# Masked columns left out of the power products of a chunked RWKV-7 inverse

## The chip, the cores and the metric

The kernel runs on one core of a Trainium2 chip. The metric is the device time of one launch in microseconds, as the median of the runs. Three runs of the kernel before took 1457.06 to 1458.89 us, with a median of 1458.34 us.

## The reference, cut to what matters

The reference is a chain of transformer layers over 256 tokens with 1024 features. The part that is changed is the RWKV-7 time mix of the first layer: 16 heads of 64 features, each with a state that is updated token by token.

```python
def step(state, inp):
    r_t, w_t, k_t, v_t, a_t, b_t = inp
    sa = jnp.einsum('bhvk,bhk->bhv', state, a_t)
    state = (state * w_t[:, :, None, :] + sa[..., None] * b_t[:, :, None, :]
             + v_t[..., None] * k_t[:, :, None, :])
    return state, jnp.einsum('bhvk,bhk->bhv', state, r_t)
```

The kernel does it in 4 chunks of 64 tokens. Within a chunk, what the tokens add to one another through `sa` is a triangular system I - A, where A is 64x64 and strictly triangular. A to the power 64 is zero, so the inverse is the product of (I + A)(I + A^2)(I + A^4) up to (I + A^32).

## The kernel before, in words

The 16 heads are worked off as 8 pairs. Of a pair, one head has partitions 0 to 63 ("upper") and the other has partitions 64 to 127 ("lower"). A tile of a pair holds 4 chunks of 64 columns, so it is 128x256.

The inverse has six levels (`power_level`, from L841). `P` is the matrix and `Q` its transpose. P is strictly upper triangular and Q strictly lower triangular.

- Level 0 squares P and Q (P = Q'P and Q = P'Q, in banks ps4 and ps5).
- Levels 1 to 3 square both again, and also multiply the running sum Z by the power (`times_z`, bank ps6). VectorE adds the product to Z (`add_z`, L2016 to L2027). ScalarE copies the new powers out of PSUM (`take_powers`, L1465 to L1473).
- Level 4 squares only Q, and multiplies Z.
- Level 5 only multiplies Z, for the upper head into bank 6 and for the lower head into bank 4.

Every product of a level is one call of `quarter` (L809): a float32 matmul of one head and one chunk with 64 rows, 64 stationary columns and 64 moving columns. An upper product uses one quarter of the array and a lower product the opposite quarter, and the code lets them alternate. The profile shows two MATMUL instructions for one float32 matmul. So level 0 is 32 instructions, levels 1 to 3 are 48 each, level 4 is 32, and level 5 is 16. `quarter` is also used for the Gram matrices (`grams`, 32 instructions of a pair) and for `scan_u` (4 instructions of a chunk).

`rwkv_phase` writes the order out by hand. Phase n has 12 slots. It scans pair n (`scan_r`, `scan_u`, `scan_state`, one in each slot), works the six levels of pair n + 1 in the slots 0, 2, 4, 6, 8 and 10, and fills in dense projection matmuls (`one_tile`, L509) between them. Slot 9 has `bonus_sum` of pair n + 2 (L798, and `spread` at L774). Slot 10 issues `scan_u` and right behind it level 5. The phase ends with `grams` of pair n + 2, which waits for level 5's sum of pair n + 1 through `z_ready`, and for the decayed keys of pair n + 2 (`bkar_ready`, L1991). VectorE and ScalarE have their own lists in the same order. Phases run from -1 to 7, and the six levels are in phases -1 to 6.

The running sum Z alternates between the two buffers `Zp`. Level 5 writes the result to `Zf[m % 2]`, which `scan_u` of the next phase reads.

Of the kernel before, what the change touches and what calls it, by code (L numbers as in the profile page):

```python
# [17 lines left out]
ALU = mybir.AluOpType  # L18
# [3 lines left out]
P = 128  # L22
S = 256
# [3 lines left out]
HD = 64  # L27
H = D // HD
PAIRS = H // 2
CH = 64  # L30
NC = S // CH
# [61 lines left out]
def build(nc, ins, out):  # L93
    weights, aux_d, const_d, small_d, rows_d, swbias_d, x_d, pos_d = ins
    with ExitStack() as ctx:
# [6 lines left out]
        ps = [ctx.enter_context(nc.psum_tensor(f"ps{i}", [P, 512], F32)) for i in range(8)]  # L102
# [35 lines left out]
        def carve(*shape):  # L138
            n = int(np.prod(shape))
            a = arena[:, top[0]:top[0] + n]  # L140
            top[0] += n
            assert top[0] <= ARENA, top[0]
            if len(shape) == 1:
                return a
            names = "abcd"[:len(shape)]
            pat = f"p ({' '.join(names)}) -> p {' '.join(names)}"
            return a.rearrange(pat, **{k: v for k, v in zip(names, shape)})

        def const(name):
            return cst[:, CO[name][0]:CO[name][1]]  # L150
# [56 lines left out]
        Sw = carve(2, CH)  # L207
        PQ0 = carve(2, NC, CH)
        PQ = [carve(2, NC, CH) for _ in range(2)]
        Zp = [carve(NC, CH) for _ in range(2)]  # L210
        Zf = [carve(NC, CH) for _ in range(2)]
        y_f, yc = pT[:, 0, 0:S], pT[:, 1, 0:S]
        yq, yn = sc[:, 0, 0:S], sc[:, 1, 0:S]
# [93 lines left out]
        pow_p, pow_q, z_mm, pq_ready, z_ready = map(sem, ("pow_p", "pow_q", "z_mm", "pq_ready", "z_ready"))  # L307
# [134 lines left out]
        def _(pe):  # L442
# [253 lines left out]
            for b in range(NB):  # L696
# [4 lines left out]
                for k in range(KT):  # L701
                    m = pe.transpose(ps[4 + k // 2][:, (k % 2) * S + b * P:(k % 2) * S + b * P + P],
                                     xn[:, b, k * P:(k + 1) * P], ident)
# [5 lines left out]
            for tile in range(2):  # L709
                for k in range(KT):  # L710
                    if tile == 0 and k % 2 == 0:
                        pe.wait_ge(hT_ready, k // 2 + 1)
                    m = pe.matmul(ps[0][:, tile * S:(tile + 1) * S], w[:, k, tile * P:(tile + 1) * P], hT[:, k, :],
                                  start=k == 0, stop=k == KT - 1)
# [4 lines left out]
            for b in range(NB):  # L719
                for k in range(KT):  # L720
                    m = pe.matmul(ps[2][:, b * 48:b * 48 + 48], hT[:, k, b * P:(b + 1) * P],
                                  w_small[:, k, 32:80], start=k == 0, stop=k == KT - 1)
# [84 lines left out]
            def quarter(dst, lhs, rhs):  # L807

                return pe.matmul(dst, lhs, rhs, start=True, stop=True)  # L809
# [29 lines left out]
            def power_level(m, lvl):  # L839

                src = PQ0 if lvl == 0 else PQ[(lvl - 1) % 2]  # L841
                p_, q_ = src[:, 0], src[:, 1]
                z_ = Zp[(lvl - 1) % 2]
                if lvl == 0:
                    pe.wait_ge(pq0_ready, m + 1)
                    pe.wait_ge(mask_done, m + 1)
                else:
                    pe.wait_ge(pq_ready, 9 * m + min(2 * lvl, 9))
                if lvl == 1:
                    pe.wait_ge(z0_ready, m + 1)  # L850
                if lvl > 1:
                    pe.wait_ge(z_ready, 5 * m + lvl - 1)
                cols = [slice(c * CH, (c + 1) * CH) for c in range(NC)]

                def square_p(half_of_rows, c):
                    return quarter(half_of_rows(ps[4])[:, cols[c]], half_of_rows(q_)[:, c, :], half_of_rows(p_)[:, c, :])

                def square_q(half_of_rows, c):
                    return quarter(half_of_rows(ps[5])[:, cols[c]], half_of_rows(p_)[:, c, :], half_of_rows(q_)[:, c, :])

                def times_z(half_of_rows, c, bank=6):
                    return quarter(half_of_rows(ps[bank])[:, cols[c]], half_of_rows(q_)[:, c, :],
                                   half_of_rows(z_)[:, c, :])

                if lvl < 4:
                    for c in range(NC):
                        square_p(upper, c)
                        square_q(lower, c)
                    for c in range(NC):
                        p_last = square_p(lower, c)  # L870
                        if lvl:
                            times_z(upper, c)
                        else:
                            q_last = square_q(upper, c)
                    p_last.then_inc(pow_p, 1)
                    if lvl:
                        for c in range(NC):
                            q_last = square_q(upper, c)
                            z_last = times_z(lower, c)
                        z_last.then_inc(z_mm, 1)  # L880
                    q_last.then_inc(pow_q, 1)
                elif lvl == 4:
                    for c in range(NC):
                        square_q(upper, c)
                        times_z(lower, c)
                    for c in range(NC):
                        q_last = square_q(lower, c)
                        z_last = times_z(upper, c)
                    q_last.then_inc(pow_q, 1)
                    z_last.then_inc(z_mm, 1)  # L890
                else:
                    for c in range(NC):
                        times_z(upper, c)
                        z_last = times_z(lower, c, bank=4)
                    z_last.then_inc(z_mm, 1)
# [121 lines left out]
            for n in range(2):  # L1017
                one_ready(ONE - 2 + n)
                w = one_pair(ONE - 2 + n, 4)
                for b in range(NB):  # L1020
                    m = split_product(ps[2 + b][:], [([t[:, 4 * n + k, b * P:(b + 1) * P] for t in g],
                                                      [t[:, k, :] for t in w]) for k in range(4)],
                                      first=n == 0, last=n == 1)
                m.then_inc(unit_done, 1)

            for w_ in range(2):
# [4 lines left out]
                for k in range(16):  # L1031
                    m = pe.matmul(ps[4][:, 60 * w_:60 * w_ + 60], w[:, k, :], blk[w_][:, k, :], start=k == 0, stop=k == 15)
# [3 lines left out]
            for g in range(GROUPS):  # L1036
                m = pe.matmul(ps[6][0:N_CMP, g * HD:(g + 1) * HD], xg[:, 1, g * N_CMP:(g + 1) * N_CMP],
                              cmp_w2[:, HD:P], start=True, stop=True)
# [5 lines left out]
            for g in range(GROUPS):  # L1044
                if g >= 1:
                    pe.wait_ge(c_arg, g)
                for b in range(NB):
                    for hh in range(HPG):
                        c = (b * HPG + hh) * N_CMP
                        m = pe.matmul(ps[0][:, c:c + N_CMP], qT[0:HD, HPG * g + hh, b * P:(b + 1) * P],  # L1050
                                      kcmp[0:HD, g * N_CMP:(g + 1) * N_CMP], start=True, stop=True)
# [4 lines left out]
                for b in range(NB):  # L1056
                    m = pe.transpose(ps[1][:, b * P:(b + 1) * P],
                                     cp_[:, b * HPG:(b + 1) * HPG, :].rearrange("p h n -> p (h n)"), ident)
# [4 lines left out]
                for b in range(NB):  # L1063
                    m = pe.matmul(ps[2][:, b * S:(b + 1) * S], cpT[:, b, :], Vblk[:, g, :], start=True, stop=True)
# [21 lines left out]
            for n in range(4):  # L1086
# [3 lines left out]
                for b in range(NB):  # L1090
                    for hf in range(2):
                        m = split_product(ps[4 + 2 * b + hf][:],
                                          [([t[:, 2 * n + k, b * P:(b + 1) * P] for t in (m_hi, m_lo)],
                                            [t[:, k, hf * 512:(hf + 1) * 512] for t in w]) for k in range(2)],
                                          first=n == 0, last=n == 3)
# [138 lines left out]
        def _(act):  # L1234
# [230 lines left out]
            def take_powers(m, lvl):  # L1465

                if lvl < 4:
                    act.wait_ge(pow_p, 4 * m + lvl + 1)
                    act.activation(PQ[lvl % 2][:, 0].rearrange("p c t -> p (c t)"), ps[4][:, 0:S],
                                   ACT.Copy).then_inc(pq_ready, 1)  # L1470
                act.wait_ge(pow_q, 5 * m + lvl + 1)
                act.activation(PQ[lvl % 2][:, 1].rearrange("p c t -> p (c t)"), ps[5][:, 0:S],
                               ACT.Copy).then_inc(pq_ready, 1)  # L1473

            def take_u(n, c):
# [229 lines left out]
        def _(dve):  # L1705
# [304 lines left out]

            def first_z(m):

                dve.tensor_tensor(Zp[0], PQ0[:, 0], const("ident2").unsqueeze(1).broadcast_to((P, NC, CH)),
                                  ALU.add).then_inc(z0_ready, 1)

            def add_z(m, lvl):  # L2016

                dve.wait_ge(z_mm, 5 * m + lvl)
                dve.drain()
                if lvl < 5:  # L2020
                    dve.tensor_tensor(Zp[lvl % 2].rearrange("p c t -> p (c t)"), ps[6][:, 0:S],
                                      Zp[(lvl - 1) % 2].rearrange("p c t -> p (c t)"), ALU.add).then_inc(z_ready, 1)
                else:
                    z = Zf[m % 2].rearrange("p c t -> p (c t)")
                    old = Zp[0].rearrange("p c t -> p (c t)")
                    dve.tensor_tensor(z[0:HD], ps[6][0:HD, 0:S], old[0:HD], ALU.add)
                    dve.tensor_tensor(z[HD:P], ps[4][HD:P, 0:S], old[HD:P], ALU.add).then_inc(z_ready, 1)  # L2027

            def take_r(n, c):

# [745 lines left out]
```

## Time and profile before

| what | value |
|---|---|
| median of the runs | 1458.34 us (1457.06 to 1458.89) |
| the profiled execution | 1458.99 us |
| its span, first to last instruction | 1457.2 us |
| mean granted TensorE clock | 0.961 |
| TensorE busy in the span | 1364.8 us (94%) |
| VectorE, ScalarE, GpSimd busy | 855.6, 634.9, 282.5 us |
| matmuls of L809 | 2176 instructions, 62.3 to 325.3 us |

1.8 us of the execution's own time lie outside its span. A busy time of TensorE is the union of its instructions, whose ends are modelled, so the distance between the starts of two groups says more than their length.

### The profile page before, as it was taken

The page shows a single profiled execution, that of the slowest core. Times are in us where ns is not written, and L with a number is a line of the kernel's source. Part 1 is how long each engine was busy: PE and PEld are TensorE (multiplying, and loading weights), DVE is VectorE, ACT ScalarE, POOL GpSimd, SP SyncE. Part 2 cuts the span into 40 slices and gives each one's busy share as a digit, 9 for nine tenths or more (in the row PEclk, how much of TensorE's full clock was granted, in tenths as well). Part 3 has the DMA queues.
Part 4 walks back from the last instruction along what each step waited for, and adds up shares of the span by engine and source line. Part 5 has one row for each costly group of instructions (what it writes and reads, how often), then busy time and mean ns, then how long its engine had stood idle before and what let it go on. Part 6 is the DMA issues. An engine that isn't in the chain of part 4 may idle for free.

```text
span 1457.2 us, 28178 instructions
## 1 busy us (share of the span) xinstructions
PE 1364.8 (94%) x10956; PEld 1209.3 (83%) x10956; DVE 855.6 (59%) x1696; ACT 634.9 (44%) x1246; POOL 282.5 (19%) x354
## 2 busy tenths in 40 slices
PE   7899999899899988999998998899999789999998
PEld 6898888789788887999888855899988656799986
DVE  5566666645568876788645345544446555544444
ACT  4344444433144435666445425543334246543343
POOL 0002322211344321132201102111200122111200
PEclk9999999999799999999998969999999989999999
DMA  7312111024321134455555401455454331255552
GB/s 291 116 60 82 67 59 60 31 88 149 117 83 59 59 131 159 175 187 186 181 194 174 162 1 58 145 181 194 173 202 145 115 116 59 87 176 193 180 189 100
DMA packets 26503, 188.87 MB, mean 130 GB/s; under 512 B 2944, under 2 KB 3072, under 8 KB 4128
## 3 DMA queue, kind: packets, MB, share of 16 engines
q1 hardware_dynamic: 25632, 182.51, 35.1%
q0 software_dynamic: 768, 4.92, 1.0%
q8 instruction: 73, 1.20, 0.3%
q14 instruction: 30, 0.25, 0.1%
HBM read 186.37 MB, written 1.05 MB: 129 GB/s over the span
## 4 chain that ended last, share of the span: by engine, by line
PE 85%; DVE 7%; ACT 4%; issue 1%; DVEq 1%; DMA 1%; POOLq 0%; POOL 0%; ACTq 0%; SPq 0%
PE ps L561 48%; PE ps L509 13%; PE ps L809 5%; PE ps L1188 2%; PE ps L660 1%; PE ps L649 1%; PE ps L1050 1%; PE ps L541 1%; PE ps L534 1%; PE ps L774 1%; PE ps L828 1%; PE ps L533 1%; PE ps L908 1%; PE ps L478 1%; DVE mx L1726 1%
## 5 line engine op out<-in xcount | busy, mean ns | idle before, releaser
L561 PE MATMUL ps<-h_hi,w_hi 128*128 128x256 f32 x1208 | 345.5, 286 | 5.0 <-DVE h_lo L1785 5.0
L561 PE MATMUL ps<-h_lo,w_hi 128*128 128x256 f32 x1208 | 344.7, 285 | 0.0
L561 PE MATMUL ps<-h_hi,w_lo 128*128 128x256 f32 x1208 | 344.5, 285 | 0.0
L1815 DVE TENSOR_TENSOR w_lo<-ring,w_hi 128x1024 fp32r<-128x1024 f32 x111 | 139.2, 1254 | 270.5 <-ACT w_hi L1315 270.4
L1315 ACT ACTIVATE w_hi<-ring 128x1024 fp32r<-128x1024 f32 x119 | 126.2, 1060 | 321.5 <-PE ps L561 321.1
L561 PEld LDWEIGHTS ps<-h_hi,w_hi 128*128 128x128 f32 x1208 | 234.8, 194 | 6.6 <-issue 6.6
L561 PEld LDWEIGHTS ps<-h_lo,w_hi 128*128 128x128 f32 x1208 | 234.8, 194 | 0.0
L561 PEld LDWEIGHTS ps<-h_hi,w_lo 128*128 128x128 f32 x1208 | 234.8, 194 | 0.0
L509 PE MATMUL ps<-oT_r,ring_r 128*128 128x256 f32 x512 | 147.3, 288 | 0.0
L1821 DVE TENSOR_TENSOR w_lo<-ring,w_hi 128x1024 fp32r<-128x1024 f32 x111 | 139.7, 1258 | 0.0
L1317 ACT ACTIVATE w_hi<-ring 128x1024 fp32r<-128x1024 f32 x119 | 124.5, 1046 | 0.0
L561 PE MATMUL ps<-w_lo,a_hi 128*128 128x512 f32 x264 | 102.8, 389 | 0.0
L561 PE MATMUL ps<-w_hi,a_hi 128*128 128x512 f32 x264 | 102.8, 389 | 0.0
L561 PE MATMUL ps<-w_hi,a_lo 128*128 128x512 f32 x264 | 102.7, 389 | 0.0
L509 PEld LDWEIGHTS ps<-oT_r,ring_r 128*128 128x128 f32 x512 | 100.5, 196 | 0.0
L2415 POOL CAST a_hi<-arena 128x256 f32 (+1 forms) x66 | 31.5, 478 | 309.2 <-DVE arena L1877 309.2
L809 PE MATMUL ps<-arena 64*64 64x64 f32 x2176 | 78.9, 222 | 3.4 <-DVE arena L2027 2.5
L809 PEld LDWEIGHTS ps<-arena 64*64 64x64 f32 x2176 | 69.0, 134 | 12.0 <-issue 3.4
L509 PE MATMUL ps<-oT_r,early_r 128*128 128x256 f32 x208 | 66.7, 321 | 2.6 <-DVE arena L2066 0.8
L2417 POOL TENSOR_TENSOR a_lo<-arena,a_hi 128x256 f32 (+1 forms) x66 | 58.4, 885 | 14.1 <-issue 13.4
L509 PE MATMUL ps<-xn_r,early_r 128*128 128x256 f32 x208 | 59.8, 288 | 0.0
L561 PEld LDWEIGHTS ps<-w_hi,a_lo 128*128 128x128 f32 x264 | 49.6, 188 | 10.3
(406 smaller groups left out, 2786.4 us busy)
## 6 DMA issues: line engine op xcount, KB each, us to landing
ring<-in_weights SPq DMA_DIRECT2D x170, 1024.0 KB, 4.8
arena<-in_aux POOLq DMA_DIRECT2D x1, 2112.0 KB, 12.7
grow<-in_rows POOLq DMA_DIRECT2D x3, 512.0 KB, 3.9
cst<-in_consts SPq DMA_DIRECT2D x1, 1497.5 KB, 14.4
x<-in_x SPq DMA_DIRECT2D x1, 1024.0 KB, 5.0
arena<-in_swbias POOLq DMA_DIRECT2D x1, 1024.0 KB, 7.7
out<-xn SPq DMA_DIRECT2D x4, 256.0 KB, 2.2
sml<-in_small SPq DMA_DIRECT2D x1, 536.0 KB, 5.6
```

Source lines behind the costliest of these rows:

```text
L478: m = pe.transpose(ps[k // 2][:, (k % 2) * S + b * P:(k % 2) * S + b * P + P], xn[:, b, k * P:(k + 1) * P], ident)
L509: mm = pe.matmul(dst, w[a][:, k, tile * P:(tile + 1) * P], rhs[b][:, k, :], start=k == 0 and a == b, stop=k == KT - 1 and a == 1)
L533: pe.matmul(bank[:, 0:P], q[:, 0:P], keys(0, P), start=True, stop=True)
L561: m = pe.matmul(dst, l[a], r[b], start=first and n == 0 and a == b, stop=last and n == len(pairs) - 1 and a == 1)
L809: return pe.matmul(dst, lhs, rhs, start=True, stop=True)
L1188: m = pe.matmul(ps[6 + h % 2][:, 0:S], w[:, k, (h % 4) * P:(h % 4 + 1) * P], cq[:, k, :], start=k == 0, stop=k == 2)
L1315: act.activation(w_hi[:, half_of(u0, m), WH:], ring[:, (u0 + m) % RING, WH:], ACT.Copy).then_inc(w_hi_p, 1)
L1317: act.activation(w_hi[:, half_of(u0, m), 0:WH], ring[:, (u0 + m) % RING, 0:WH], ACT.Copy).then_inc(w_hi_d, 1)
L1815: dve.tensor_tensor(w_lo[:, half_of(u0, m), WH:], ring[:, (u0 + m) % RING, WH:], w_hi[:, half_of(u0, m), WH:].bitcast(F32), ALU.subtract). ...
L1821: dve.tensor_tensor(w_lo[:, half_of(u0, m), 0:WH], ring[:, (u0 + m) % RING, 0:WH], w_hi[:, half_of(u0, m), 0:WH].bitcast(F32), ALU.subtrac ...
L2415: pool.tensor_copy(a_hi[:, m, :], act_f[:, j % 2, :])
L2417: pool.tensor_tensor(a_lo[:, m, :], act_f[:, j % 2, :], a_hi[:, m, :].bitcast(F32), ALU.subtract).then_inc(act_split, 1)
```

## The change

1. `times_z` of level l leaves out the first 2^l moving columns of each chunk, where the product is zero. It streams 62, 60, 56, 48 and 32 columns at the levels 1 to 5, in place of 64.
2. At level 5 it also takes only rows 32 to 63 and stationary columns 0 to 31 of each head, so that the matmul is 32 rows by 32 stationary columns by 32 moving columns.
3. `square_p` at level 3 streams only columns 32 to 63 of P. `square_q` at level 4 has stationary columns 32 to 63 of P and streams columns 0 to 31 of Q; it writes to partitions 32 to 63 of the head.
4. ScalarE copies only the computed half of P at level 3 and of Q at level 4.
5. The running sum is kept in `Zf[m % 2]` throughout and is added to in place; `Zp` is gone. `add_z` adds only the computed columns, and at level 5 only 32 rows of each head.

No instruction is added or removed on any engine, and every wait and signal stays where it was.

```diff
-        Zp = [carve(NC, CH) for _ in range(2)]
...
-                z_ = Zp[(lvl - 1) % 2]
+                z_ = Zf[m % 2]
+                z0 = 1 << lvl
...
                 def square_p(half_of_rows, c):
-                    return quarter(half_of_rows(ps[4])[:, cols[c]], half_of_rows(q_)[:, c, :], half_of_rows(p_)[:, c, :])
+                    t0 = CH // 2 if lvl == 3 else 0
+                    return quarter(half_of_rows(ps[4])[:, c * CH + t0:(c + 1) * CH], half_of_rows(q_)[:, c, :],
+                                   half_of_rows(p_)[:, c, t0:CH])
 
                 def square_q(half_of_rows, c):
+                    if lvl == 4:
+                        return quarter(half_of_rows(ps[5])[CH // 2:CH, c * CH:c * CH + CH // 2],
+                                       half_of_rows(p_)[:, c, CH // 2:CH], half_of_rows(q_)[:, c, 0:CH // 2])
                     return quarter(half_of_rows(ps[5])[:, cols[c]], half_of_rows(p_)[:, c, :], half_of_rows(q_)[:, c, :])
 
                 def times_z(half_of_rows, c, bank=6):
-                    return quarter(half_of_rows(ps[bank])[:, cols[c]], half_of_rows(q_)[:, c, :],
-                                   half_of_rows(z_)[:, c, :])
+                    if lvl == 5:
+                        return quarter(half_of_rows(ps[bank])[0:CH // 2, c * CH + z0:(c + 1) * CH],
+                                       half_of_rows(q_)[CH // 2:CH, c, 0:CH // 2],
+                                       half_of_rows(z_)[CH // 2:CH, c, z0:CH])
+                    return quarter(half_of_rows(ps[bank])[:, c * CH + z0:(c + 1) * CH], half_of_rows(q_)[:, c, :],
+                                   half_of_rows(z_)[:, c, z0:CH])
...
-                act.activation(PQ[lvl % 2][:, 1].rearrange("p c t -> p (c t)"), ps[5][:, 0:S],
+                n = CH // 2 if lvl == 4 else CH
+                act.activation(PQ[lvl % 2][:, 1, :, 0:n], ps[5][:, 0:S].rearrange("p (c t) -> p c t", c=NC)[:, :, 0:n],
                                ACT.Copy).then_inc(pq_ready, 1)
...
+                new = [ps[bank][:, 0:S].rearrange("p (c t) -> p c t", c=NC)[:, :, z0:CH] for bank in (6, 4)]
                 if lvl < 5:
-                    dve.tensor_tensor(Zp[lvl % 2].rearrange("p c t -> p (c t)"), ps[6][:, 0:S],
-                                      Zp[(lvl - 1) % 2].rearrange("p c t -> p (c t)"), ALU.add).then_inc(z_ready, 1)
+                    dve.tensor_tensor(z[:, :, z0:CH], new[0], z[:, :, z0:CH], ALU.add).then_inc(z_ready, 1)
                 else:
-                    z = Zf[m % 2].rearrange("p c t -> p (c t)")
-                    old = Zp[0].rearrange("p c t -> p (c t)")
-                    dve.tensor_tensor(z[0:HD], ps[6][0:HD, 0:S], old[0:HD], ALU.add)
-                    dve.tensor_tensor(z[HD:P], ps[4][HD:P, 0:S], old[HD:P], ALU.add).then_inc(z_ready, 1)
+                    for rows, part in ((slice(0, CH // 2), new[0]), (slice(HD, HD + CH // 2), new[1])):
+                        ins = dve.tensor_tensor(z[rows, :, z0:CH], part[rows], z[rows, :, z0:CH], ALU.add)
+                    ins.then_inc(z_ready, 1)
```

## Rows read from the trace of the kernel before

**Rows 1.** The page: busy time, and the chain that ended last, by line.
```profile
PE 1364.8 (94%) x10956; PEld 1209.3 (83%) x10956; DVE 855.6 (59%) x1696; ACT 634.9 (44%) x1246; POOL 282.5 (19%) x354
...
PE ps L561 48%; PE ps L509 13%; PE ps L809 5%; PE ps L1188 2%; PE ps L660 1%; PE ps L649 1%; PE ps L1050 1%; PE ps L541 1%; PE ps L534 1%; PE ps L774 1%; PE ps L828 1%; PE ps L533 1%; PE ps L908 1%; PE ps L478 1%; DVE mx L1726 1%
```

**Rows 2.** Busy time by stage, all engines; first column the stage.
```profile
core 0: us, PE busy (x) PEld busy (x) DVE busy (x) ACT busy (x) POOL busy (x), PEclk, DMA share, GB/s
...
120.00:150.00 30.00, 29.87 (x443) 26.77 (x443) 20.26 (x48) 13.87 (x36) 8.30 (x12) 1.00 0.21 72
...
270.00:300.00 30.00, 26.43 (x451) 23.40 (x447) 13.09 (x38) 9.13 (x29) 5.58 (x11) 1.00 0.09 28
...
sum 265.00, PE 257.76 PEld 229.50 DVE 170.83 ACT 112.02 POOL 55.26; mean PE 28.64 PEld 25.50 DVE 18.98 ACT 12.45 POOL 6.14
```

**Rows 3.** Timeline of TensorE, phase 1: start us, length us, line, count.
```profile
129.62 0.33 PE L809 MATMUL ps<-arena 64*64 64x64 f32 x4
129.88 0.70 PE L757 MATMUL ps<-pT,cst 128*128 128x256 f32 x2
...
131.71 1.62 PE L809 MATMUL ps<-arena 64*64 64x64 f32 x48
133.26 0.39 PE L509 MATMUL ps<-oT_r,early_r 128*128 128x256 f32 x1
133.48 0.28 PE L509 MATMUL ps<-xn_r,early_r 128*128 128x256 f32 x1
133.60 0.28 PE L509 MATMUL ps<-oT_r,ring_r 128*128 128x256 f32 x1
...
135.69 0.28 PE L509 MATMUL ps<-oT_r,ring_r 128*128 128x256 f32 x1
135.90 1.73 PE L809 MATMUL ps<-arena 64*64 64x64 f32 x52
137.55 0.39 PE L509 MATMUL ps<-oT_r,early_r 128*128 128x256 f32 x1
...
146.82 1.15 PE L809 MATMUL ps<-arena 64*64 64x64 f32 x32
147.90 0.38 PE L509 MATMUL ps<-oT_r,hT_r 128*128 128x256 f32 x1
...
149.73 0.60 PE L774 MATMUL ps<-cst,arena 128*128 128x128 f32 x4
150.09 0.36 PE L509 MATMUL ps<-oT_r,hT_r 128*128 128x256 f32 x1
...
150.98 0.79 PE L809 MATMUL ps<-arena 64*64 64x64 f32 x20
151.70 0.39 PE L509 MATMUL ps<-oT_r,hT_r 128*128 128x256 f32 x1
```

**Rows 4.** Timeline of TensorE, matmuls with other widths.
```profile
20.25 3.64 PE L718 MATMUL ps<-hT,sml 128*32 128x256 f32 x16
23.82 4.08 PE L721 MATMUL ps<-sml,hT 128*128 128x48 f32 x32
...
139.92 0.50 PE L767 MATMUL ps<-cst,arena 128*128 128x2 f32 x4
140.28 0.36 PE L509 MATMUL ps<-oT_r,early_r 128*128 128x256 f32 x1
```

**Rows 5.** Who waited for whom, TensorE's waits, 62 to 327 us.
```profile
PE ps L809 <- DVE arena L2027: 2.5, 2, 2.2
```

**Rows 6.** Timeline of VectorE at the end of phase 5.
```profile
274.25 0.42 DVE L1984 TENSOR_TENSOR arena<-ps,arena 128x256 f32<-128x256 f32 x1 [0.44 <-PE ps L774]
...
276.89 0.43 DVE L2027 TENSOR_TENSOR arena<-ps,arena 64x256 f32<-64x256 f32 x1
```

**Rows 7.** Groups by line and shape, 62 to 327 us.
```profile
L2032 DVE COPY arena<-ps 128x64 f32<-128x64 f32 x32 | 7.2, 225 | 25.5 <-PE ps L908 25.5
...
L2013 DVE TENSOR_TENSOR arena<-arena,cst 128x256 f32<-128x256 f32 x8 | 3.4, 427 | 0.7
...
L1472 ACT ACTIVATE arena<-ps 128x256 f32<-128x256 f32 x40 | 15.5, 388 | 18.4 <-PE ps L809 16.7
```

More of the change, by code:

```diff
@@ L1467, in take_powers @@
                 if lvl < 4:
+                    t0 = CH // 2 if lvl == 3 else 0
                     act.wait_ge(pow_p, 4 * m + lvl + 1)
-                    act.activation(PQ[lvl % 2][:, 0].rearrange("p c t -> p (c t)"), ps[4][:, 0:S],
+                    act.activation(PQ[lvl % 2][:, 0, :, t0:CH], ps[4][:, 0:S].rearrange("p (c t) -> p c t", c=NC)[:, :, t0:CH],
                                    ACT.Copy).then_inc(pq_ready, 1)
                 act.wait_ge(pow_q, 5 * m + lvl + 1)
-                act.activation(PQ[lvl % 2][:, 1].rearrange("p c t -> p (c t)"), ps[5][:, 0:S],
+                n = CH // 2 if lvl == 4 else CH
+                act.activation(PQ[lvl % 2][:, 1, :, 0:n], ps[5][:, 0:S].rearrange("p (c t) -> p c t", c=NC)[:, :, 0:n],
                                ACT.Copy).then_inc(pq_ready, 1)
@@ L2011, in first_z @@
             def first_z(m):
-                dve.tensor_tensor(Zp[0], PQ0[:, 0], const("ident2").unsqueeze(1).broadcast_to((P, NC, CH)),
+                dve.tensor_tensor(Zf[m % 2], PQ0[:, 0], const("ident2").unsqueeze(1).broadcast_to((P, NC, CH)),
                                   ALU.add).then_inc(z0_ready, 1)
@@ L2019, in add_z @@
                 dve.drain()
+                z = Zf[m % 2]
+                z0 = 1 << lvl
+                new = [ps[bank][:, 0:S].rearrange("p (c t) -> p c t", c=NC)[:, :, z0:CH] for bank in (6, 4)]
                 if lvl < 5:
-                    dve.tensor_tensor(Zp[lvl % 2].rearrange("p c t -> p (c t)"), ps[6][:, 0:S],
-                                      Zp[(lvl - 1) % 2].rearrange("p c t -> p (c t)"), ALU.add).then_inc(z_ready, 1)
-                else:
-                    z = Zf[m % 2].rearrange("p c t -> p (c t)")
-                    old = Zp[0].rearrange("p c t -> p (c t)")
-                    dve.tensor_tensor(z[0:HD], ps[6][0:HD, 0:S], old[0:HD], ALU.add)
-                    dve.tensor_tensor(z[HD:P], ps[4][HD:P, 0:S], old[HD:P], ALU.add).then_inc(z_ready, 1)
+                    dve.tensor_tensor(z[:, :, z0:CH], new[0], z[:, :, z0:CH], ALU.add).then_inc(z_ready, 1)
+                else:
+                    for rows, part in ((slice(0, CH // 2), new[0]), (slice(HD, HD + CH // 2), new[1])):
+                        ins = dve.tensor_tensor(z[rows, :, z0:CH], part[rows], z[rows, :, z0:CH], ALU.add)
+                    ins.then_inc(z_ready, 1)
             def take_r(n, c):
```

## The prediction

> **What bounds the kernel now.** The page comes first. TensorE is busy for 94% of the span, and the chain that ended last runs mostly over its matmuls; the products that are changed, L809, hold 5% of that chain [rows 1]. The share of the whole says little about one stage, so the windows from 62 to 327 us come next, where all L809 instructions lie. TensorE is busy there for 257.8 of 265 us, and in 120 to 150 us for 29.87 of 30 us, at a granted clock of 1.00, which is 2.4 GHz. VectorE is busy for 171 us and ScalarE for 112 us [rows 2]. So what TensorE gains or loses in the levels moves the end by as much, except where it waits for another engine. The list of waits shows two waits of L809 for level 5's sum (L2027), 2.5 us in all, 2.2 us of it in one place [rows 5].
>
> **What a group of quarter matmuls costs.** The timeline of phase 1 holds groups of the same matmul in several counts. I measure from the start of a group to the start of the next line. 4 instructions take 0.26 us (129.62 to 129.88), 20 take 0.72, 32 take 1.08, 48 take 1.55 and 52 take 1.65 us [rows 3]. That is a straight line. From 4 to 52 the slope is (1.65 - 0.26) / 48 = 0.029 us, and 0.144 us is left over per group. The upper and lower quarters run side by side, so in one quarter an instruction takes 0.058 us.
>
> **What limits the 0.058 us.** A float32 matmul that streams 256 columns over 32 stationary ones takes 3.57 / 16 = 0.223 us (20.25 to 23.82) [rows 4], or 0.87 ns a column, so 64 columns stream in 0.056 us. The load of 64 stationary columns is a second limit of the same size. The proof is L767: four instructions that stream only 2 columns, over 128 stationary ones, take 0.36 us to the next start, exactly as four of L774 that stream 128 [rows 3, 4]. With 64 stationary columns half of that load is left. So a matmul that streams fewer columns and still loads 64 keeps its 0.058 us. Only fewer stationary columns as well make it shorter.
>
> **What the 0.144 us per group are.** They appear where the tile shape changes, with or without a wait for a semaphore. L509 instructions start 0.12 us apart. From the last of them to L809 it is 0.21 us (135.69 to 135.90), 0.09 us more. The first L509 behind L809 then takes 0.22 us (133.26 to 133.48) until the next, 0.10 us more: its load of 128 columns is not hidden [rows 3]. Where the shape stays (L774 to L509 at 150.09) four instructions take 0.36 us with none of it [rows 3]. So a change of tile shape costs some 0.094 us during which TensorE empties, and then an exposed load: 0.10 us for 128 stationary columns, 0.05 for 64, 0.025 for 32.
>
> **Level 4.** Its code lets `square_q` and `times_z` alternate in both loops. Before, both were 64x64 and the level was one group, 1.08 us (146.82 to 147.90) [rows 3]. Now `square_q` has 32 stationary columns and goes to partitions 32 to 63 of a head, which only a tile 32 columns wide fits, while `times_z` stays at 64. So each of the 16 matmuls has another shape than the one before it. A 64x64 matmul alone (two instructions in one quarter) costs 0.26 us, as the group of 4 does, less 16 columns of the last stream at 0.87 ns: 0.25. The narrow one costs 2 x 0.029 + 0.094 + 0.025 = 0.18. The level becomes 8 x (0.25 + 0.18) = 3.44 us, 2.36 more. The slot-9 and slot-10 work behind it on TensorE, VectorE and GpSimd is only late by that. Eight pairs: **+18.9 us**.
>
> No row has a change between 64 and 32 stationary columns, or between tiles in opposite quarters. The nearest are those between 64 and 128 [rows 3]. Below, the cost is zero, if opposite quarters need not empty. Above, a narrow matmul costs no less than the wide one's 0.26, which gives 8 x 0.51 - 1.08 = 3.0 us a level, 24 in all. With 0.15 for the narrow and 0.23 for the wide it is 2.0 a level, 16 in all. I take 18.9, since every change of shape that I read has its 0.09 us.
>
> The Trainium skill, TensorEngine Tiling (Array Packing), Key Properties, has the rule: "Changing tiling mode (not just tile) drains the TensorE". It makes no exception for tiles in other quarters. By it the 16 changes are paid; without it level 4 would keep its 1.08 us. The trace agrees for every change of shape that it shows.
>
> **Level 5.** All its matmuls are now 32x32, so they stay one group, of 8 x 0.029 + 0.094 + 0.025 = 0.35 us. Before, its 16 instructions took 0.61 us alone. In the seven phases with a scan they follow `scan_u` without a change of shape, 0.72 us together [rows 3]; now it is 0.26 + 0.35 = 0.61. Saved: 0.26 + 7 x 0.11 = **1.0 us**. Bounds: a saving of 1.9 us without the new change of shape; a loss of 0.9 if 32 stationary columns load no faster (7 x 0.12).
>
> The Trainium skill, on the same page under Instruction Overhead, says that a matmul has about 60 cycles of overhead, so that one column takes as long as 60. By it level 5 would gain nothing from its 32 columns, and my sum would end 2 us higher.
>
> **Levels 1 to 3.** 62, 60 and 56 moving columns, and 32 in level 3's `square_p`, all over 64 stationary ones: nothing, by L767 [rows 4]. At most the last stream of a group is shorter, 8 columns or 0.01 us.
>
> **VectorE and ScalarE.** ScalarE's copy of 128x256 takes 0.388 us [rows 7]; with half the columns at two levels it gets shorter. A copy by VectorE of 128x64 takes 0.225 and an add of 128x256 0.427 [rows 7], about 1.05 ns a column, so level 4's add saves 0.07 us and level 5's two adds 0.13 each. All this lies beside TensorE's fill work, and is worth nothing except where TensorE waits for L2027. At the end of phase 5 that chain runs on VectorE from L1984 (274.25, released by L774 of slot 9) to L2027 [rows 6], and the two waits [rows 5] get shorter by 0.27 us each: **-0.5 us**. As L774 comes behind level 4, the 2.36 us pass through this chain too. Without any of these savings the sum is 0.5 higher.
>
> **One buffer.** `add_z` already waited for the level's products, and the next level for the sum, so no wait is new. `first_z` writes `Zf` of the pair two back, whose last `scan_u` ended a phase earlier. It costs nothing; if it waited, VectorE's slack would cover it, and uncovered it is a 0.43 us add per pair, 3.4 us.
>
> **Sum.** 18.9 - 1.0 - 0.5 = 17.4 us on the profiled 1458.99, or 1476.4. That execution was 0.65 above the median of the runs, so the median becomes 1458.34 + 17.4 = **1475.7 us**, 1.2% slower. The later stages move as a block; their transfers follow TensorE's signals.
>
> **Rivals.**
> *Opposite quarters don't empty each other* (chance 0.15). Level 4 then keeps the pace of its wide matmuls, 1.08 us, and level 5 saves 8 x 8 x 0.029 = 1.9 us; with the 0.5 us that is 1455.9, 0.17% faster. It decides if a change costs under 0.02 us (16 x 8 x 0.02 = 2.4). For it speaks that no row shows such a pair; against it, that no change of shape in the trace is free.
> *Time follows the streamed columns* (0.05), the other side. Of 7168 columns in six levels, 1008 are left out: 14% of 224 x 0.029 = 6.5 us, 0.9 a pair, 7.3 in all: 1451.0. L767 speaks against it [rows 4].
> *The clock falls behind the thin level 4* (0.04). Under 1.00 a matmul takes twice as long; 1.5 us lost in each phase bring 12 us more, 1488. Phase 5, with little fill, had 1.00 throughout [rows 2].
>
> **How the numbers follow.** The forecast has 0.76, with a range of its own of 1470 to 1481: 16 us with all savings, to 24 with none. It misses that perhaps one time in ten. Reaching down to the second case, 1455 to 1482 leaves out under 0.2. A change under 0.2% (2.9 us) can't be told from none. Slower: 0.76 + 0.04, less a rest: 0.79. Within 0.2%: most of the first rival, 0.12. Faster: 0.09.
>
> **What the profile after would show.** Level 4 as 16 groups of two instructions, some 0.25 and 0.18 us apart, and 3.4 us from the first to what follows; if it still takes about 1.1 us the step on shape changes is wrong. Level 5 as one 32x32 group of 0.35 us, 0.26 behind the start of `scan_u`. Levels 1 to 3 at 1.55 us as before; less would show that the load doesn't bind. Phases 2.2 us longer each. The wait for L2027 some 0.3 us shorter.

## The result, and the profile after

The changed kernel took 1482.72 us, median of 4 runs (1481.8 to 1486.07), against 1457.70 for the kernel before. The ratio is 1.0178, with a 95% interval of 1.0158 to 1.0197: 25 us slower. The forecast was 1475.7 us with a range of 1455 to 1482. The direction was right; the size was outside the range. The profiled execution took 1486.07 us, with a span of 1484.3 us.

The page of the changed kernel, its section of costliest groups, shows the change in one line. L808 is `quarter`, one line higher than before:

```profile
L808 PE MATMUL ps<-arena 64*64 64x64 f32 (+6 forms) x2176 | 97.6, 221 | 2.5 <-DVE arena L2038 2.0
```

The count is the same, 2176 instructions, but the busy time has grown from the 78.9 us of L809 on the page before to 97.6 us, although no matmul is larger. The groups of the stage, kept apart by shape, show in which matmuls:

```profile
L808 PE MATMUL ps<-arena 64*64 64x64 f32 x1280 | 64.0, 225 | 2.5 <-DVE arena L2038 2.0 <-DVE arena L2044 0.4
...
L808 PE MATMUL ps<-arena 64*64 64x48 f32 x128 | 20.5, 241 | 0.0
L808 PE MATMUL ps<-arena 64*32 64x32 f32 x128 | 15.9, 205 | 0.0
...
L808 PE MATMUL ps<-arena 64*64 64x32 f32 x128 | 9.0, 219 | 0.0
L808 PE MATMUL ps<-arena 64*64 64x56 f32 x128 | 9.0, 221 | 0.0
...
L808 PE MATMUL ps<-arena 32*32 32x32 f32 x128 | 3.7, 199 | 0.0
```

The two shapes of level 4, 64x48 and 64*32, hold 36.4 us for 256 instructions, and so 0.14 us each. The two of level 3 hold 18.0 us for as many. The mean length of one is much the same (205 to 241 ns); what differs is how far they overlap. A reader who looks only at the mean would miss it.

The timeline of TensorE, phase 1, shows level 4 and what comes behind it. Its group is named after its first form; it holds both.

```profile
151.43 3.40 PE L808 MATMUL ps<-arena 64*32 64x32 f32 x32
154.76 0.39 PE L508 MATMUL ps<-oT_r,hT_r 128*128 128x256 f32 x1
...
156.05 1.12 PE L797 MATMUL ps<-arena,cst 128*128 128x256 f32 x2
156.97 1.06 PE L773 MATMUL ps<-cst,arena 128*128 128x128 f32 x4
...
158.25 0.41 PE L508 MATMUL ps<-oT_r,ring_r 128*128 128x256 f32 x1
158.47 0.41 PE L508 MATMUL ps<-oT_r,hT_r 128*128 128x256 f32 x1
...
159.24 0.85 PE L808 MATMUL ps<-arena 64*64 64x64 f32 x20
160.02 0.38 PE L508 MATMUL ps<-oT_r,hT_r 128*128 128x256 f32 x1
```

Level 4 takes 3.33 us to the next start, where it took 1.08 [rows 3]. And from 156 us on, the dense L508 matmuls start 0.22 us apart instead of 0.12: the granted clock is 0.57 between 156 and 160 us, so TensorE runs at 1.2 GHz for most of that time. Windows that each reach from one phase's `grams` to the next show how often. Before (first fence) and after (second):

```profile
120.85:153.77 32.92, 32.92 (x480) 29.47 (x480) 22.35 (x53) 14.32 (x38) 8.30 (x12) 1.00 0.19 66
153.77:186.69 32.92, 32.92 (x481) 29.46 (x480) 22.34 (x53) 14.33 (x38) 8.35 (x12) 1.00 0.19 66
```

```profile
125.45:162.09 36.64, 36.64 (x481) 32.20 (x480) 21.93 (x53) 14.12 (x38) 8.26 (x12) 0.95 0.17 59
162.09:200.03 37.94, 37.94 (x481) 33.34 (x480) 21.93 (x53) 14.12 (x38) 8.31 (x12) 0.91 0.16 58
200.03:235.12 35.09, 35.09 (x481) 30.89 (x480) 21.93 (x53) 14.12 (x38) 8.27 (x12) 1.00 0.17 61
```

The phase with the clock at 1.00 is 35.09 - 32.92 = 2.17 us longer. It is the 2.2 us a phase that was forecast. The others lose 1.55 and 2.85 us on top, with a granted clock of 0.95 and 0.91. So there are two costs: the matmuls of level 4, and a clock that falls behind them. In phase 2 it falls already inside level 4 (at 190.3 us, of 188.06 to 191.93). A phase is named here by the pair that it scans: phase 1 has level 4 at 151 us, phase 2 at 188 us.

### The profile page after: what moved, and what is told of

Read it like the earlier page. It is cut to its first block, busy times and chain, and to the rows that moved or that the text cites. A ratio compares the mean times of both kernels' runs of the same rounds, so it can differ in the third digit from the quotient of the medians.

```text
span 1484.3 us, 28178 instructions
## 1 busy us (share of the span) xinstructions
PE 1393.7 (94%) x10956; PEld 1230.6 (83%) x10956; DVE 852.1 (57%) x1696; ACT 633.5 (43%) x1246; POOL 283.7 (19%) x354
## 4 chain that ended last, share of the span: by engine, by line
PE 85%; DVE 7%; ACT 4%; DMA 2%; issue 1%; DVEq 1%; POOLq 0%; POOL 0%; SPq 0%; ACTq 0%
PE ps L560 47%; PE ps L508 14%; PE ps L808 6%; PE ps L1197 2%; DMA ring<-in_weights 2%; PE ps L659 1%; PE ps L648 1%; PE ps L773 1%; PE ps L827 1%; PE ps L1059 1%; PE ps L540 1%; PE ps L533 1%; PE ps L532 1%; PE ps L917 1%; PE ps L477 1%
## 5 line engine op out<-in xcount | busy, mean ns | idle before, releaser
L508 PE MATMUL ps<-oT_r,ring_r 128*128 128x256 f32 x512 | 148.5, 290 | 0.0
L508 PEld LDWEIGHTS ps<-oT_r,ring_r 128*128 128x128 f32 x512 | 102.2, 200 | 0.0
L808 PE MATMUL ps<-arena 64*64 64x64 f32 (+6 forms) x2176 | 97.6, 221 | 2.5 <-DVE arena L2038 2.0
L808 PEld LDWEIGHTS ps<-arena 64*64 64x64 f32 (+1 forms) x2176 | 81.7, 132 | 17.6 <-DVE arena L2002 2.1
L508 PE MATMUL ps<-oT_r,early_r 128*128 128x256 f32 x208 | 65.4, 315 | 3.0 <-ACT arena L1420 0.8
L508 PE MATMUL ps<-oT_r,hT_r 128*128 128x256 f32 x176 | 58.8, 334 | 1.3 <-issue 1.3
L508 PE MATMUL ps<-xn_r,early_r 128*128 128x256 f32 x208 | 58.7, 282 | 0.0
```

The costliest lines, as they stand in the source:

```text
L508: mm = pe.matmul(dst, w[a][:, k, tile * P:(tile + 1) * P], rhs[b][:, k, :], start=k == 0 and a == b, stop=k == KT - 1 and a == 1)
```

## The experiments

Each experiment edits the changed kernel, except for the drains, which edit the kernel before, and the two kernels that are measured once more as they are. The ratios are to runs of the kernel before that were made together with each group of experiments: a median of 1458.06 us for the first four, 1457.98 for the next three, and 1459.20 for the last three.

**Level 4's square of Q as it was.**

```diff
                 def square_q(half_of_rows, c):
-                    if lvl == 4:
-                        return quarter(half_of_rows(ps[5])[CH // 2:CH, c * CH:c * CH + CH // 2],
-                                       half_of_rows(p_)[:, c, CH // 2:CH], half_of_rows(q_)[:, c, 0:CH // 2])
                     return quarter(half_of_rows(ps[5])[:, cols[c]], half_of_rows(p_)[:, c, :], half_of_rows(q_)[:, c, :])
...
-                n = CH // 2 if lvl == 4 else CH
+                n = CH
```

> The changed kernel with one part undone: level 4's square of Q is again 64 rows by 64 stationary columns by 64 moving columns, and ScalarE copies it whole. All else of the change stays. Theory (alternating tile shapes at level 4 empty TensorE 16 times a level, and TensorE's thin work there lets the granted clock fall): level 4 is one group again, 1.08 us in place of 3.33; no stretch at 1.2 GHz inside the stage of the levels; level 5 keeps its 0.37 us; the time is 1456 to 1457 us, 0.1% under the kernel before. Rival (the clock fell for another reason, the in-place sum or the 32x32 matmuls of level 5): level 4 goes back but some stretches at 1.2 GHz stay, 1460 to 1465 us.

Measured: 1459.99 us, ratio 1.0004 (0.9992 to 1.0016), the same as before. The timeline of this kernel has level 4 back at 1.08 us, and `scan_u` with the 32x32 level 5 at 0.64:

```profile
144.17 1.15 PE L808 MATMUL ps<-arena 64*64 64x64 f32 x32
145.25 0.38 PE L508 MATMUL ps<-oT_r,hT_r 128*128 128x256 f32 x1
...
148.32 0.70 PE L808 MATMUL ps<-arena 64*64 64x64 f32 x20
148.96 0.39 PE L508 MATMUL ps<-oT_r,hT_r 128*128 128x256 f32 x1
```

So one part of the change, the narrow `square_q` with its copy, carries all of its cost. The expected gain of 1 to 2 us was missed, and the profile had one stretch of lower clock at the end of phase 5, against "none" in the expectation. Between 273 and 281 us, where TensorE is busy for 5.9 of 8 us, its granted clock is 0.57.

**Level 4 in two groups.**

```diff
                     for c in range(NC):
                         square_q(upper, c)
-                        times_z(lower, c)
+                        q_last = square_q(lower, c)
                     for c in range(NC):
-                        q_last = square_q(lower, c)
+                        times_z(lower, c)
                         z_last = times_z(upper, c)
```

> The changed kernel with level 4 in another order: first the eight narrow squares (upper and lower alternating, all of them 64x32), then the eight products with Z (all 64x64). One change of shape inside the level in place of 15. Theory (the cost is per change of shape, not per narrow matmul): 8 x 0.029 + 0.12 for the squares and 8 x 0.058 + 0.13 for the products, so the level takes 0.95 us, 0.13 less than in the kernel before; no stretch at 1.2 GHz; 1455 to 1456.5 us, the fastest of all. Rival (a 64x32 matmul into partitions 32 to 63 is dear by itself): the level stays above 2 us and the time above 1465 us.

Measured: 1455.52 us, ratio 0.9984 (0.9970 to 0.9999). The same narrow matmuls in another order, and the level takes 0.97 us (146.32 to 147.29):

```profile
146.32 1.04 PE L808 MATMUL ps<-arena 64*32 64x32 f32 x32
147.29 0.39 PE L508 MATMUL ps<-oT_r,hT_r 128*128 128x256 f32 x1
```

A narrow matmul is not dear, then; the change between two shapes is. The 0.97 us is below the level's 1.08 of before.

**Level 4 in pairs.**

```diff
                     for c in range(NC):
                         square_q(upper, c)
-                        times_z(lower, c)
-                    for c in range(NC):
                         q_last = square_q(lower, c)
+                        times_z(lower, c)
                         z_last = times_z(upper, c)
```

> The changed kernel with level 4 in pairs: the squares of the upper and the lower head, then the two products with Z, chunk after chunk. 7 changes of shape inside the level in place of 15, the same matmuls. Theory (per change of shape): 4 x (0.18 + 0.25) = 1.7 us a level, 0.65 over the kernel before, so 5.2 us for eight levels, less 1.5 for level 5 and the shorter adds: 1461 us if the clock holds at 2.4 GHz; each stretch at 1.2 GHz adds about 1.5 us, and fewer of them than the eight of the changed kernel are expected. Rival (per narrow matmul): the level is as long as in the changed kernel, 3.3 us, and the time 1482 us.

Measured: 1461.58 us, ratio 1.0030 (1.0018 to 1.0043), as expected. The level takes 1.72 us, and the stage has a clock of 1.00:

```profile
145.79 1.79 PE L808 MATMUL ps<-arena 64*32 64x32 f32 x32
147.51 0.39 PE L508 MATMUL ps<-oT_r,hT_r 128*128 128x256 f32 x1
```

**A control for the clock: drains, no shapes.** This edits the kernel before. All matmuls stay 64x64x64.

```diff
                     for c in range(NC):
                         square_q(upper, c)
+                        pe.drain()
                         times_z(lower, c)
+                        pe.drain()
                     for c in range(NC):
                         q_last = square_q(lower, c)
+                        pe.drain()
                         z_last = times_z(upper, c)
+                        pe.drain()
```

> The kernel before, with TensorE's queue emptied by a drain after each of the 16 matmuls of level 4; all stay 64x64x64, no shape changes, no column is left out. It is a control for the clock. Theory (the clock falls because TensorE does little for 3 us, whatever the cause): each matmul alone takes at least 0.26 us, so level 4 takes 4 to 6 us, and stretches at 1.2 GHz follow it in most of the eight phases as in the changed kernel; 1485 to 1510 us. Rival (the clock falls because of the changes of shape or the narrow tiles): the level is as long, but the stage stays at 2.4 GHz.

Measured: 1523.72 us, ratio 1.0444 (1.0413 to 1.0476), above the 1485 to 1510 expected. The level takes 6.9 us, more than the 4 to 6 expected. Its last 1.8 us are already at 1.2 GHz; until then a matmul starts every 0.40 us, which makes 6.4 us for the 16. The clock falls without any change of shape; the windows view over its whole stage says 0.90 and the dense matmuls behind level 4 are 0.21 us apart:

```profile
60.00:390.00 330.00, 313.17 (x3778) 264.59 (x3778) 168.40 (x404) 111.58 (x291) 55.14 (x87) 0.90 0.15 51
```

```profile
161.57 6.80 PE L809 MATMUL ps<-arena 64*64 64x64 f32 x32
...
168.85 0.41 PE L509 MATMUL ps<-xn_r,hT_r 128*128 128x256 f32 x1
169.06 0.41 PE L509 MATMUL ps<-oT_r,ring_r 128*128 128x256 f32 x1
```

So the clock falls with thin work that has no change of shape in it, and it held through the seven changes of a level in pairs, which is over in 1.72 us: the shapes are not its cause. "Thin" means here that matmuls start seldom: the 32 instructions of a level 4 start within 3.33 or 6.9 us, where they started within 1.08.

**Only the shorter streams.** Both changes of tile undone: the edit of the first experiment, and level 5's special case taken out too. It keeps the shorter streams, the narrower adds and the single buffer.

```diff
                 def times_z(half_of_rows, c, bank=6):
-                    if lvl == 5:
-                        return quarter(half_of_rows(ps[bank])[0:CH // 2, c * CH + z0:(c + 1) * CH],
-                                       half_of_rows(q_)[CH // 2:CH, c, 0:CH // 2],
-                                       half_of_rows(z_)[CH // 2:CH, c, z0:CH])
                     return quarter(half_of_rows(ps[bank])[:, c * CH + z0:(c + 1) * CH], half_of_rows(q_)[:, c, :],
                                    half_of_rows(z_)[:, c, z0:CH])
```

> The changed kernel with both tile changes undone: level 4's square of Q and level 5's product are again 64 rows by 64 stationary columns. What stays is the shorter streams (62, 60, 56, 48, 32 columns and 32 in level 3's square of P), the narrower adds and copies, and the sum in one buffer. Theory (the load of 64 stationary columns sets the pace): every group of the levels keeps its time to 0.01 us, also level 5 with its 32 moving columns at 0.61 us alone and 0.72 us behind the scan's matmul; 1457 to 1459 us, no difference that can be measured. Rival (time follows the streamed columns): level 5 shrinks by a third and level 4 by a tenth, and the time is 3 us or more under the kernel before.

Measured: 1458.25 us, ratio 0.9996 (0.9977 to 1.0014). Level 4 with its 48 columns takes 1.08 us. Level 5 with half the columns takes 0.69 with `scan_u`, against 0.72 [rows 3]; the shorter last stream accounts for that.

```profile
147.62 0.77 PE L808 MATMUL ps<-arena 64*64 64x64 f32 x20
148.31 0.39 PE L508 MATMUL ps<-oT_r,hT_r 128*128 128x256 f32 x1
```

**Half of level 4 alternating.**

```diff
-                    for c in range(NC):
-                        q_last = square_q(lower, c)
-                        z_last = times_z(upper, c)
+                    for c in range(0, NC, 2):
+                        for d in (c, c + 1):
+                            q_last = square_q(lower, d)
+                        for d in (c, c + 1):
+                            z_last = times_z(upper, d)
```

> The changed kernel with level 4's second half in runs of two: the first four squares and products alternate as in the changed kernel, the last eight go square, square, product, product. The two matmuls of a run lie in one quarter and don't overlap. Theory (per change of shape, and the clock by how thin the work is and for how long): the first half takes 1.67 us as in the changed kernel, the second 2 x (0.24 + 0.37) = 1.2 us, so level 4 is 2.9 us in place of 3.33, with 11 changes in place of 15; 14 us over the kernel before by the matmuls alone, 1472 us, and a few stretches at 1.2 GHz still, fewer than the changed kernel's seven: 1473 to 1478 us. Rival (the clock falls at any alternation): seven stretches as before, 1479 to 1480 us.

Measured: 1476.92 us, ratio 1.0135 (1.0104 to 1.0165), inside the expected 1473 to 1478. The level takes 2.86 us (expected 2.9), and the clock of the stage is 0.97:

```profile
151.38 2.93 PE L808 MATMUL ps<-arena 64*32 64x32 f32 x32
154.24 0.39 PE L508 MATMUL ps<-oT_r,hT_r 128*128 128x256 f32 x1
```

**Level 4 cut up by dense work.**

```diff
                     for c in range(NC):
                         square_q(upper, c)
                         times_z(lower, c)
+                        if c == 2:
+                            between()
                     for c in range(NC):
+                        if c == 2:
+                            between()
                         q_last = square_q(lower, c)
                         z_last = times_z(upper, c)
...
-                        power_level(n + 1, slot // 2)
+                        power_level(n + 1, slot // 2, between=lambda: next(fill, None))
...
-                    next(fill, None)
+                    if not (powers and slot in (8, 9)):
+                        next(fill, None)
```

> The changed kernel with level 4 cut in three parts of 6, 6 and 4 matmuls and the two fills of dense projection matmuls that followed in the slots 8 and 9 put between the parts. The matmuls of level 4 and their alternation stay, so the changes of shape stay (two of them are now to and from the dense matmuls). Theory (my sum lacked only the clock, which falls after three us of thin work in one piece): the stage stays at 2.4 GHz but for phase 5, which has no fill; level 4's cost remains 18 us, and the time is 1474 to 1477 us, about what the prediction's sum gave. Rival (the cost is not the clock's, but of the changes alone): the time stays at 1482 us.

Measured: 1489.68 us, ratio 1.0226 (1.0190 to 1.0262). As a version this is a miss, 13 us above the end of what was expected. The windows of its profile explain a part of it:

```profile
62.00:262.00 200.00, 197.46 (x2713) 173.93 (x2712) 123.76 (x292) 80.93 (x211) 38.86 (x60) 1.00 0.19 65
262.00:355.00 93.00, 86.49 (x1079) 73.76 (x1078) 43.01 (x114) 29.14 (x82) 16.15 (x28) 0.89 0.13 47
```

Up to 262 us, through phases -1 to 3, the clock does stay at 1.00, where the changed kernel had 0.95 or less in most phases. From there on it is 0.89, and the lack of fill in phase 5 is not the whole reason. It falls first in phase 4, inside level 4 (259.67 to 266.01), although the dense matmuls do lie between the level's parts; they are 0.22 us apart from the second fill on:

```profile
261.82 1.45 PE L808 MATMUL ps<-arena 64*32 64x32 f32 x12
...
263.58 0.41 PE L508 MATMUL ps<-xn_r,hT_r 128*128 128x256 f32 x1
263.80 0.41 PE L508 MATMUL ps<-oT_r,ring_r 128*128 128x256 f32 x1
```

So cutting the level up did not rule the fall out, and whether it makes it rarer rests on one profile. The three parts take 1.25, 1.25 and 0.83 us at full clock, together the 3.33 us of before. And TensorE now waits for level 5's sum in more phases (the list of waits has 4.4 us in 6 waits, against 2.0 in one), since less dense work is left between level 4 and `grams`:

```profile
PE ps L808 <- DVE arena L2043: 4.4, 6, 2.0
```

**The two kernels once more.**

> The changed kernel once more, unaltered, for a second profile. Theory (18.0 us of level 4's changes of shape less 1.4 for level 5 and the adds, the rest is time at 1.2 GHz in the stage): every level 4 at full clock takes 3.33 us again; stretches at 1.2 GHz lie again behind level 4 in most phases, 17 to 35 us in all, at places that may differ; median 1482 to 1484 us. Rival (the seven stretches were that one execution's): fewer than three stretches in the stage.

> The kernel before once more, unaltered, for a second profile, as the control for the clock. Theory: the stage of the levels has no stretch at 1.2 GHz, or one at the end of phase 5, where TensorE waits without fill, as two of the experiments had; phases 0 to 4 have none; ratio 1.000 within 0.002. Rival (stretches come by chance anywhere in the stage): some lie in the phases 0 to 4.

The changed kernel took 1488.20 us, ratio 1.0186 (1.0169 to 1.0203); the ratio repeats, while the median lies above the 1482 to 1484 expected. Two of the windows of this second profile, phases 1 and 2, show that the clock need not fall in the same phases: phase 1 kept 1.00 this time.

```profile
130.00:165.00 35.00, 35.00 (x484) 30.81 (x482) 21.94 (x53) 14.12 (x38) 8.27 (x12) 1.00 0.17 62
165.00:202.00 37.00, 37.00 (x494) 32.54 (x490) 21.97 (x54) 14.15 (x39) 8.31 (x12) 0.95 0.17 59
```

The kernel before took 1458.42, ratio 0.9993 (0.9984 to 1.0002). Its second profile has a clock of 1.00 from 120 to 270 us, and 0.91 from 270 to 290:

```profile
120.00:270.00 150.00, 148.81 (x2226) 132.63 (x2223) 104.92 (x253) 68.04 (x183) 38.96 (x57) 1.00 0.18 65
270.00:290.00 20.00, 16.43 (x261) 14.25 (x260) 8.80 (x26) 5.18 (x15) 2.89 (x6) 0.91 0.01 2
```

So the end of phase 5, where TensorE waits, can lose its clock in the kernel before too. The version with level 4's square as it was, and the one with only the shorter streams (its stage has 0.99), lost it there as well. A fall at that place alone is therefore no effect of the change.

**The two groups once more.**

> The version with level 4 in two groups once more, with more rounds, since its gain of 0.16% lay at the edge of what was measured. Theory: level 4 at 0.97 us, level 5 at 0.37 us, 0.9 + 0.9 + 0.5 us saved by row, so a ratio of 0.998 to 0.999. Rival (the gain was chance): 1.000.

Measured: 1455.85 us over 12 runs, ratio 0.9977 (0.9967 to 0.9988). It is the one version that beats both kernels, by 0.2%: 3.4 us by the medians. The rows account for 0.9 at level 4, 0.8 at level 5 and 0.5 in the waits; the rest is inside the interval.

## Why the prediction was wrong

**Right: the pace of a quarter matmul.** That its load of 64 stationary columns holds it at 0.058 us, however few it streams, stood on L767. The run with only the shorter streams measured it: no group of 64 stationary columns changed by more than 0.03 us. The rival "time follows the streamed columns" falls.

**Right: the change of shape.** Level 4 was worked out at 3.44 us and took 3.33, and 0.97 in two groups, 1.72 in pairs, 2.86 half alternating. So 18.0 us of the change are 8 x (3.33 - 1.08). In the trace of the changed kernel a wide matmul starts 0.175 us behind the narrow one, and the next narrow one 0.242 us behind that; the sum had 0.18 and 0.25. The trace before had no pair of shapes in opposite quarters; here such a pair does not overlap either. The rule of the Trainium skill that a change of tiling mode drains TensorE (TensorEngine Tiling (Array Packing), Key Properties) agrees with this: the level with 15 changes inside it takes 2.25 us more than the one without. No exception for opposite quarters shows, and the rival built on one falls.

**Right: level 5 and the waits.** 0.37 us was measured for 0.35, and 0.63 with `scan_u` for 0.61. In phase 5 the two take 0.76 us before and after, so 0.24 + 6 x 0.09 = 0.8 us are saved for 1.0. Level 5's two adds on VectorE take 0.58 us where they took 0.84, as the sum had it. TensorE's waits for them shrank from 2.5 us in two places to 2.0 in one; in phase 5 from 2.2 to 2.0. The Trainium skill (TensorEngine Tiling (Array Packing), Instruction Overhead) has the rule that one column takes as long as 60. What the prediction drew from it, that level 5 would gain nothing from its 32 columns, did not come true: 0.61 us became 0.37. The rule itself is not tested by that, since the loaded columns were halved with the streamed ones.

**Wrong: the clock at 2.4 GHz in the sum.** The sum held TensorE at 1.00 throughout and left the fall of the clock to a rival with a chance of 0.04. It happened behind or inside level 4 in seven of the eight phases that have one in the first profile, and in six in the second, and the whole miss is of that size. (The fall of phase 5 in the first profile comes only at 299.5 us, where TensorE has waited, and so where the kernel before can have one too.) With the matmuls alone as measured, the sum is 18.0 - 1.3 = 16.7 us on the 1457.7 of this comparison, or 1474.4; the run had 1482.7. The 8.3 us between are set beside the stage's granted clock, from the windows view of each kernel over its stage. Time at 1.2 GHz is summed over the clock's record in the trace of the one profiled execution; twice what the clock lacks to 1.00, times the length of the stage, gives the same within some 3 us.

| kernel | level 4 at full clock, us | clock of the stage | at 1.2 GHz, us | over before, medians, us | by the matmuls, us | left over, us | stage longer, profiled, us | left over in it, us |
|---|---|---|---|---|---|---|---|---|
| two groups | 0.97 | 1.00 | 0 | -2.5 | -2.2 | -0.3 | -2.1 | 0.1 |
| in pairs | 1.72 | 1.00 | 0 | 3.5 | 3.8 | -0.3 | 3.9 | 0.1 |
| half alternating | 2.86 | 0.97 | 17 | 18.9 | 12.9 | 6.0 | 20.1 | 7.2 |
| changed | 3.33 | 0.95 | 31 | 25.0 | 16.7 | 8.3 | 29.6 | 12.9 |
| changed, again | 3.33 | 0.94 | 34 | 29.0 | 16.7 | 12.3 | 29.6 | 12.9 |
| drains, no shapes | 6.4 | 0.90 | 68 | 65.7 | 42.6 | 23.1 | 67.2 | 24.6 |

"By the matmuls" is 8 x (level 4 - 1.08), less 1.3 for level 5 and the waits where the kernel has them. The last two columns compare the profiled executions over the stage alone: from the start of the first group of 48 to the start of the last `scan_u`. Before (first fence) that is 253.8 us, in the changed kernel (second) 283.4:

```profile
71.33 1.61 PE L809 MATMUL ps<-arena 64*64 64x64 f32 x48
...
325.14 0.33 PE L809 MATMUL ps<-arena 64*64 64x64 f32 x4
```

```profile
69.22 1.61 PE L808 MATMUL ps<-arena 64*64 64x64 f32 x48
...
352.58 0.33 PE L808 MATMUL ps<-arena 64*64 64x64 f32 x4
```

Where the clock holds, the arithmetic is right to 0.3 us. Where it falls, what is left over grows with the time at 1.2 GHz: by the medians some 0.3 us for each, and in the profiled stages, where clock and time are of the same execution, 0.36 to 0.42. Phase 1, with 1.55 us for a clock of 0.95 over 36.64 us and so for about 3.7 us, agrees with the latter. In the kernel before, whose second profile has 3.4 us at 1.2 GHz, the stage is 1.4 us longer than in its first.

The rival's place and its mechanism were right, its chance was not. Its price, 12 us for 1.5 us in each phase, had no row behind it; that it lies close to the 12.9 us left over in the profiled stages is luck, as phase 3 lost nothing and phase 2 lost 2.85. The reason given against it was that phase 5, with little fill, had 1.00 throughout. One profile was too little for that: the second one of the same kernel has 0.91 there. And the range closed at 1482 by leaving that rival out. The sum's range of its own, 1470 to 1481, does not follow from its terms either: 16 us less 2.4 for all savings gives 1471.9, and 24 us gives 1482.3. That the run came so close to the latter says nothing for it, since a narrow matmul cost 0.175 us and not the 0.26 assumed there.

**What stays open.** Why the version cut up by dense work took 1489.7 us. Its profiled execution (1486.5) has the clock back in the phases -1 to 3 and loses it from phase 4 on, 20 us in all; its waits for level 5's sum are 2.4 us longer; its stage is 0.5 us shorter than the changed kernel's. Its four executions took 1486.5, 1486.6, 1492.7 and 1493.3 us, and the two longer ones had a mean granted clock of 0.951 and 0.948 over the whole, against 0.958 in the other two. So a lower clock goes with them, but where it fell, no profile shows. The version therefore does not confirm the price of the clock, which rests on the table and on the phases. Nor does any run say why a level 4 of the same length loses the clock in one phase and keeps it in another.

## What to carry to other kernels

Before narrowing a small matmul, read which of its two operands sets its pace: here 64 loaded columns cost 0.058 us whether 64 or 32 were streamed, and only fewer loaded columns helped. A narrower tile is worth having only if all matmuls of that shape are issued together; alternating two shapes cost 2.25 us in a level of 1.08, and the same matmuls in two groups gained 0.11. When a change stretches thin work on TensorE inside dense work, as level 4 here from 1.08 to 3.33 us, price the dense work behind it at half clock as well, and take more than one profile before ruling that out. In this kernel the clock held behind a level of 1.72 us, and fell behind one of 2.86 us in some phases.

## What the runs showed of the hardware that was not expected

A drain of TensorE's queue between matmuls is dearer than a change of tile shape. With 16 drains a matmul took 0.40 us at full clock; with 15 changes of shape in a level of 3.33 us it took 0.21. The granted clock went to 1.2 GHz in phases whose busy share of TensorE never fell: phase 1 of the changed kernel is busy for 36.64 of 36.64 us, with a clock of 0.95. The Trainium skill (TensorE: Matmul & The Clock Gate, Part 1: The HAM clock gate) says that activity releases the throttle. The profile's busy time can't be read for it: this trace has the clock at 1.2 GHz behind a level 4 that the profile counts as busy throughout.
